# Taking one modulation row off TensorE: multiplied on ScalarE, added on GpSimd

## The chip, the cores and the metric

One core of one Trainium2 chip runs the kernel. It has five engines with an instruction queue each: TensorE (PE in the profile, its weight loads PEld), VectorE (DVE), ScalarE (ACT), GpSimd (POOL) and SyncE (SP), which only issues DMAs here. They share an on-chip memory, SBUF, and TensorE sums into another, PSUM. The engines order their work by semaphores alone. The metric is the device time of one execution in microseconds (us).

## The reference

One layer of a diffusion backbone, for 128 context tokens and 256 latent tokens together, width 2048. Cut to what matters here:

```
def modulation(cvec, w_mod, b_mod):
    m = jax.nn.silu(cvec) @ w_mod + b_mod           # w_mod: 2048 x 12288
    return m.reshape(cvec.shape[0], N_MOD, 1, D_MODEL)

def trunk_layer(x, mod, ...):
    hn = rmsnorm(x, g[0]) * (1.0 + mod[:, 1]) + mod[:, 0]
    z = hn @ w_in                                   # then convolutions, RG-LRU scans, gates
    m = jnp.concatenate([lru_out, sc_out], axis=-1) @ w_out
    x = x + mod[:, 2] * m
    hn = rmsnorm(x, g[1]) * (1.0 + mod[:, 4]) + mod[:, 3]
    f = (jax.nn.silu(hn @ w_gate) * (hn @ w_up)) @ w_down
    x = x + mod[:, 5] * f
```

There are two conditioning vectors (context and latent), so the modulation is a product of 2 x 2048 with 2048 x 12288. It is bound by reading 96 MB of weights, not by arithmetic.

## The kernel before

**Tokens and weights.** All 384 tokens are the columns of every large matmul. Each large weight matrix is worked off in blocks of 1024 columns of SBUF. A block is loaded by SP into a `raw` tile, rounded to `w_hi` on ScalarE (`round_blocks`, L633), its remainder `w_lo = raw - w_hi` is formed on VectorE (`subtract_blocks`, L967), and TensorE makes 24 matmuls of it (L1583 to L1585: hi*hi, hi*lo, lo*hi). Four blocks of `w_hi`/`w_lo` exist, so ScalarE may be at most four blocks ahead: it waits for `block_done`, TensorE for `lo_ready`. Eight blocks make a step.

**The stretch of this case.** Steps are counted as in the code: steps 1 to 7 are part of the input product, step 8 (i = 0) to step 11 (i = 3) are the four output steps, the product with `w_out`. After block 3 and after block 7 of an output step a pair of 128-row tiles is finished. VectorE adds it to the residual stream (`residual_pair`, L1377), ScalarE squares it (`square_pair`, L821), and VectorE adds the squares up (`add_pair`, L1386 and L1387). In ScalarE's program a square stands between the rounding of blocks: r0 r1, square, r2 r3 r4 r5, square, r6 r7. So the rounding of block 6 waits behind a square, and that behind the residual of the pair that TensorE finished last.

**The modulation beside it.** The 12288 columns of `w_mod` are 24 rows of 512 (`m`). Rows 8 to 23 are summed while the large products run, in three ways:

- On TensorE: `mod_units`. One unit is a load of 1 MB (issued by GpSimd, L570) and four matmuls of 512 columns that lie beside each other in the array (`mod_matmuls`, L1613). Row 8 to 11 are 16 such units, rows 14, 16 and 18 (`PE_ROWS`) four units each; one unit stands behind block 3 and one behind block 7 of a step. Row 18 stands in steps 9 and 10. Rows 20 to 22 (`late_mods`) come after it.
- On VectorE: `SIDE_ROWS`, six rows, each as four units of eight instructions (`side_half`, L988: `sums = rows * cond + sums`, 128x512), put between the subtractions of `w_lo` by `SIDE_AT` (`subtract_beside`). Steps 9 and 10 hold three units each, step 11 one. Their loads are also issued by GpSimd (L585). A finished row of partial sums is added up over the partitions by TensorE (`sum_side`, L1664, four matmuls of 256 columns).
- Every row is then copied (`copy_row`), turned (`turn_row`: four matmuls, L1692, or two, L1684, for a side row) and gets its bias (`add_bias`), in the order of `EVENTS`.

GpSimd's program is one queue of DMA issues; each first waits until its buffer is free. VectorE's, ScalarE's and TensorE's programs are equally strict in order.

Of the kernel before, what the change touches and what calls it, by code (L numbers as in the profile page):

```python
# [63 lines left out]
def build(nc, x_prompt, x_sample, state_rglru, c, c_ctx, w_mod, b_mod, norm_g, w_in, lru_conv_w, lru_conv_b,  # L64
# [57 lines left out]
    PE_ROWS = [MOD_FIRST + 4 + r for r in (2, 4, 6)]  # L122
# [6 lines left out]
    SIDE_OPS = 8  # L129
    N_X3 = KT  # L130
# [15 lines left out]
    with ExitStack() as ctx:  # L146
# [110 lines left out]
        side_summed = sem("side_summed")  # L257
        zeroed = sem("zeroed")
# [135 lines left out]
        def side_sums(part):  # L394

            at = 8 * T if part == 5 else 2 * BANK * (part - 3)
            home = token_rows[:] if part < 3 else scratch[:, at:at + 2 * BANK]
            return home.rearrange("p (a n) -> p a n", a=2)

# [140 lines left out]
        def _(pool):  # L540
# [45 lines left out]

            load_gates(0)
# [6 lines left out]
            for step in range(1, HEADS + OUT_STEPS - 1):  # L594
# [3 lines left out]
                if len(units) == 3:  # L598
                    load_side(units[1])
# [6 lines left out]
                load_mod(7 + 2 * step)  # L606
            load_side(SIDE_UNITS - 1)
            for unit in range(LATE_UNITS):
# [3 lines left out]
                elif LATE_SLOTS[unit] == 0:  # L612
                    pool.wait_ge(mod_used, LATE_USED)
                elif LATE_SLOTS[unit] < 3:
                    pool.wait_ge(side_step, SIDE_OPS * (SIDE_UNITS - 2 + LATE_SLOTS[unit]))
                else:
                    pool.wait_ge(act_ready, 2 * (KT // 2))
# [8 lines left out]
        def _(act):  # L626
# [195 lines left out]

            def out_step(n, i, first):
# [27 lines left out]
            with act.Fori(1, OUT_STEPS) as i:  # L851
# [103 lines left out]
        def _(dve):  # L955
# [45 lines left out]
            def copy_row(event):  # L1001

                m = EVENTS[event]
                if m in SIDE_ROWS:
                    dve.wait_ge(side_summed, SIDE_ROWS.index(m) + 1)
# [10 lines left out]
            def add_bias(event):  # L1016
# [9 lines left out]
                elif m in SIDE_ROWS:  # L1026
# [553 lines left out]
        def _(pe):  # L1580
# [77 lines left out]
            def sum_side(part):  # L1658

                sums = side_sums(part)  # L1660
                pe.wait_ge(side_step, 4 * SIDE_OPS * (part + 1))
                pe.wait_ge(mod_ready, LEAD_COUNT + EVENTS.index(SIDE_ROWS[part]))
# [15 lines left out]
            def turn_row(event):  # L1678
# [3 lines left out]
                if EVENTS[event] in SIDE_ROWS:  # L1682
# [13 lines left out]
            def usual(step):  # L1696

                def after(b):
# [7 lines left out]
                    if b % 4 == 3 and step:  # L1706
# [316 lines left out]
```

## Time and profile before

| what | value |
|---|---|
| time, median of 3 runs | 1750.77 us (1750.06 to 1751.92) |
| the profiled execution: its own time | 1751.09 us |
| the profiled execution: its span | 1749.3 us |
| TensorE busy | 1710.8 us of the span |
| VectorE, ScalarE, GpSimd busy | 945.4, 609.8, 63.3 us |
| output steps, as TensorE runs them | about 465 to 613 us of the span |

The span is the time from the first to the last instruction of the profiled execution; its own time is 1.8 us more. The start of a row is what places matmuls: their ends are modelled, and they overlap, so the distance of two starts is what an instruction costs TensorE. A percentage or a busy time of a whole run says little about one stage, so what follows looks at the stretch from 485 to 613 us.

### The profile page before, as it was taken

The numbers are of one execution on the slowest core, as the hardware profiler recorded it, in microseconds if no ns is written. First come the engines' busy times: TensorE is split into PE (matmuls) and PEld (weight loads), VectorE is DVE, ScalarE is ACT, GpSimd is POOL, SyncE is SP. The second block draws the span as 40 slices with busy tenths as digits, with TensorE's granted clock in tenths as the row PEclk, the third lists the DMA queues.
The fourth block names the chain that finished last, engine by engine and source line by source line (L and its number), as shares of the span: only waits on it lengthen the run. The fifth ranks groups of instructions, "written<-read, shape, count | busy, mean of one in ns | idle before, by whom it ended". The sixth has DMA issues, their size and how long they took to land.

```text
span 1749.3 us, 24522 instructions
## 1 busy us (share of the span) xinstructions
PE 1710.8 (98%) x10063; PEld 1632.9 (93%) x10063; DVE 945.4 (54%) x1405; ACT 609.8 (35%) x701; POOL 63.3 (4%) x99
## 2 busy tenths in 40 slices
PE   5999999999999999999999999999999999999997
PEld 3678999999899979999999999999999999999997
DVE  4446678777778578343534434353534435353445
ACT  3333455456523253222222222323232222223235
POOL 2000100110010110000000000000000000000000
PEclk8999999999999999999999999999999999999999
DMA  9996655576677876343334333433333334333421
GB/s 362 379 358 223 239 207 199 201 239 206 212 241 268 289 254 228 121 134 132 120 120 135 129 120 121 136 127 120 121 136 127 120 123 137 124 120 122 141 74 73
DMA packets 206268, 307.56 MB, mean 176 GB/s; under 512 B 5500, under 2 KB 151216, under 8 KB 203776
## 3 DMA queue, kind: packets, MB, share of 16 engines
q1 hardware_dynamic: 189472, 237.07, 40.2%
q0 software_dynamic: 16528, 69.63, 11.1%
q8 instruction: 43, 0.70, 0.2%
q14 instruction: 17, 0.14, 0.0%
q10 hardware_dynamic: 208, 0.02, 0.0%
HBM read 303.55 MB, written 3.15 MB: 175 GB/s over the span
## 4 chain that ended last, share of the span: by engine, by line
PE 94%; DMA 2%; DVE 2%; ACT 1%; issue 0%; SPq 0%; ACTq 0%; DVEq 0%
PE psum L1583 30%; PE psum L1585 29%; PE psum L1584 29%; PE psum L1613 1%; DMA raw<-in_w_mod 1%; DMA scratch<-in_w_in 1%; PE psum L1627 1%; PE psum L1605 1%; PE psum L1638 0%; DVE scratch L1182 0%; PE psum L1920 0%; PE psum L1692 0%; DVE stage L1123 0%; DVE act_lo L1399 0%; ACT scratch L668 0%
## 5 line engine op out<-in xcount | busy, mean ns | idle before, releaser
L967 DVE TENSOR_TENSOR w_lo<-raw,w_hi 128x1024 fp32r<-128x1024 f32 x364 | 444.2, 1224 | 643.3 <-ACT w_hi L633 642.8
L1583 PE MATMUL psum<-act_hi,w_hi 128*128 128x384 f32 x2304 | 775.0, 336 | 5.6 <-DVE act_lo L1139 3.3
L1585 PE MATMUL psum<-act_hi,w_lo 128*128 128x384 f32 x2304 | 770.6, 334 | 0.0
L1584 PE MATMUL psum<-act_lo,w_hi 128*128 128x384 f32 x2304 | 770.4, 334 | 0.0
L633 ACT ACTIVATE w_hi<-raw 128x1024 fp32r<-128x1024 f32 x364 | 381.6, 1058 | 790.8 <-PE psum L1585 718.6
L1583 PEld LDWEIGHTS psum<-act_hi,w_hi 128*128 128x128 f32 x2304 | 432.8, 188 | 35.0 <-issue 25.8
L1584 PEld LDWEIGHTS psum<-act_lo,w_hi 128*128 128x128 f32 x2304 | 433.0, 188 | 0.0
L1585 PEld LDWEIGHTS psum<-act_hi,w_lo 128*128 128x128 f32 x2304 | 432.9, 188 | 0.0
L1583 PE MATMUL psum<-h_hi,w_hi 128*128 128x384 f32 x704 | 235.8, 335 | 0.9 <-DVE h_lo L1443 0.9
L1585 PE MATMUL psum<-h_hi,w_lo 128*128 128x384 f32 x704 | 235.2, 334 | 0.0
L1584 PE MATMUL psum<-h_lo,w_hi 128*128 128x384 f32 x704 | 235.2, 334 | 0.0
L1583 PEld LDWEIGHTS psum<-h_hi,w_hi 128*128 128x128 f32 x704 | 132.1, 188 | 1.2 <-DVE h_lo L1443 1.2
L1584 PEld LDWEIGHTS psum<-h_lo,w_hi 128*128 128x128 f32 x704 | 132.2, 188 | 0.0
L1585 PEld LDWEIGHTS psum<-h_hi,w_lo 128*128 128x128 f32 x704 | 132.1, 188 | 0.0
L1452 DVE SCALAR_TENSOR_TENSOR xT<-psum,modT,xT 128x128 f32<-128x128 f32 x352 | 122.1, 410 | 6.8 <-PE psum L1585 6.7
L988 DVE SCALAR_TENSOR_TENSOR token_rows<-raw,cond,token_rows 128x512 f32<-128x512 f32 x90 | 61.6, 745 | 0.0
L988 DVE SCALAR_TENSOR_TENSOR scratch<-stage,cond,scratch 128x512 f32<-128x512 f32 x62 | 42.4, 746 | 0.0
L1627 PE MATMUL psum<-raw,cond_w 128*32 128x512 f32 (+1 forms) x288 | 36.3, 593 | 4.7 <-DMA raw<-in_w_mod 4.7
L866 ACT ACTIVATE h_hi<-stage 128x768 fp32r<-128x768 f32 x22 | 18.6, 847 | 51.6 <-DVE stage L1438 51.6
L821 ACT ACTIVATE scratch<-xT 128x768 f32 (+1 forms) x8 | 6.8, 847 | 79.9 <-DVE xT L1377 79.9
L1117 DVE TENSOR_TENSOR w_lo<-scratch,w_hi 128x768 fp32r<-128x768 f32 x16 | 15.1, 955 | 26.8 <-ACT w_hi L654 26.8
L654 ACT ACTIVATE w_hi<-scratch 128x768 fp32r<-128x768 f32 x16 | 13.2, 836 | 39.9 <-DMA scratch<-in_w_in 36.8
(189 smaller groups left out, 758.4 us busy)
## 6 DMA issues: line engine op xcount, KB each, us to landing
raw<-in_w_mod POOLq DMA_DIRECT2D x50, 1024.0 KB, 6.1
raw<-in_w_gate SPq DMA_DIRECT2D x44, 1024.0 KB, 5.0
raw<-in_w_up SPq DMA_DIRECT2D x44, 1024.0 KB, 5.0
raw<-in_w_down SPq DMA_DIRECT2D x44, 1024.0 KB, 5.0
raw<-in_w_in SPq DMA_DIRECT2D x34, 1024.0 KB, 5.2
raw<-in_w_mod SPq DMA_DIRECT2D x32, 1024.0 KB, 9.4
raw<-in_w_out SPq DMA_DIRECT2D x16, 1024.0 KB, 5.5
stage<-in_w_mod POOLq DMA_DIRECT2D x14, 1024.0 KB, 6.5
```

The costliest lines, as they stand in the source:

```text
L633: act.activation(split_view(w_hi, b), source, ACT.Copy).then_inc(hi_ready, 1)
L866: act.activation(h_hi[:, 2 * pair:2 * pair + 2, :], silu_g[:, 2 * pair:2 * pair + 2, :], ACT.Copy)\
L967: dve.tensor_tensor(split_view(w_lo, b), source, split_view(w_hi, b).bitcast(F32), ALU.subtract).then_inc(lo_ready, 1)
L988: dve.scalar_tensor_tensor(sums[:, a, :], rows[:, j, :], cond[:, a, k:k + 1], sums[:, a, :], ALU.mult, ALU.add).then_inc(side_step, 1)
L1117: dve.tensor_tensor(w_lo[k % SLOTS][:, 0:X_WIDE], x_raw[k % 2], w_hi[k % SLOTS][:, 0:X_WIDE].bitcast(F32), ALU.subtract).then_inc(lo_ready, 1)
L1452: last = dve.scalar_tensor_tensor(xT[:, k, start:end], psum[:, down_banks[j] + a, start:end], modT[:, 5 * KT + k, seg:seg + 1], xT[:, k, s ...
L1583: pe.matmul(psum[:, bank, 0:T], hi, x_hi, start=first, stop=False)
L1584: pe.matmul(psum[:, bank, 0:T], hi, x_lo, start=False, stop=False)
L1585: return pe.matmul(psum[:, bank, 0:T], lo, x_hi, start=False, stop=last)
L1605: out = pe.matmul(psum[32 * j:32 * j + 32, MOD_BANK, :], cond_w[:, k, :], rows[:, 512 * j:512 * j + 512], start=k == 0, stop=k == KT - 1, ...
L1613: out = pe.matmul(psum[32 * j:32 * j + 32, MOD_BANK, :], cond_w[:, 4 * q + j, :], rows[:, j, :], start=q == 0, stop=q == 3, tile_position= ...
L1627: out = pe.matmul(psum[32 * j:32 * j + 32, MOD_BANK, 0:tiles * P], cond_w[:, depth * unit + i, :], rows[:, i, :], start=unit == 0 and i < ...
```

## The change

Row 18 leaves `PE_ROWS` and becomes `SHARED_ROW`. Its eight loads of 512 KB (two of 16 k each) are issued by ScalarE. ScalarE multiplies each piece by the conditioning values (`scale_shared`: four activations of 128x512 with a per-partition scale for each of eight groups, 32 in all), GpSimd adds the products into `shared_sums` (`add_shared`: four additions of 128x512 a group, two for the first, 30 in all), and TensorE adds up over the partitions as for a side row. Group g + 2 is loaded when group g has been multiplied; group g + 1 is multiplied when group g has been added. In steps 9 and 10 the four `mod_units` fall away. GpSimd's additions stand in its queue between the loads of the side rows. Row 18 is turned in the short form. ScalarE's loop over the output steps is written out.

```
-    PE_ROWS = [MOD_FIRST + 4 + r for r in (2, 4, 6)]
+    PE_ROWS = [MOD_FIRST + 4 + r for r in (2, 4)]
+    SHARED_ROW = MOD_FIRST + 4 + 6
+    SUM_ORDER = SIDE_ROWS[:4] + [SHARED_ROW] + SIDE_ROWS[4:]
...
+        shared_raw = [stage[:, (4 + b) * BLOCK:(5 + b) * BLOCK].rearrange("p (k n) -> p k n", n=512) for b in (0, 1)]
+        shared_scaled_rows = stage[:, 0:2 * BLOCK].rearrange("p (k a n) -> p k a n", k=2, a=2)
+        shared_sums = scratch[:, 4 * BANK:6 * BANK].rearrange("p (a n) -> p a n", a=2)
...
+            def add_shared(group):
+                for k in range(2):
+                    if group == 0 and k == 0:
+                        continue
+                    for a in range(2):
+                        pool.wait_ge(shared_scaled, scaled_until(group) + 2 * k + a + 1)
+                        done = added_until(group) + (2 * k if group else 0) + a
+                        if done >= 2:
+                            pool.wait_ge(shared_added, done - 1)
+                        pool.tensor_tensor(shared_sums[:, a, :], shared_sums[:, a, :], shared_scaled_rows[:, k, a, :],
+                                           ALU.add).then_inc(shared_added, 1)
...
-            for step in range(1, HEADS + OUT_STEPS - 1):
+            for step in range(1, HEADS + 1):
...
+            load_side(13)
+            load_side(14)
+            add_shared(0)
+            add_shared(1)
+            add_shared(2)
+            load_side(15)
+            add_shared(3)
+            load_side(16)
+            add_shared(4)
+            load_side(17)
+            add_shared(5)
+            add_shared(6)
+            load_side(18)
+            add_shared(7)
             load_side(SIDE_UNITS - 1)
...
+            def load_shared(group):
+                if group < 2:
+                    act.wait_ge(act_ready, KT // 2 + 4)
+                else:
+                    act.wait_ge(shared_scaled, scaled_until(group - 1))
+                act.dma_start(shared_raw[group % 2],
+                              w_mod_v[:, 2 * group:2 * group + 2, SHARED_ROW * 512:SHARED_ROW * 512 + 512])\
+                    .then_inc(shared_landed[group % 2], 16)
+
+            def scale_shared(group):
+                if group == 0:
+                    act.wait_ge(act_ready, 2 * (KT // 2))
+                    act.wait_ge(head_done, HEADS)
+                else:
+                    act.wait_ge(shared_added, added_until(group))
+                act.wait_ge(shared_landed[group % 2], 16 * (group // 2 + 1))
+                for k in range(2):
+                    for a in range(2):
+                        to = shared_sums[:, a, :] if group == 0 and k == 0 else shared_scaled_rows[:, k, a, :]
+                        at = 2 * group + k
+                        act.activation(to, shared_raw[group % 2][:, k, :], ACT.Copy, scale=cond[:, a, at:at + 1])\
+                            .then_inc(shared_scaled, 1)
+                if group + 2 < SHARED_GROUPS:
+                    load_shared(group + 2)
...
                 else:
                     round_blocks("GM", n, range(0, 2))
+                    if i < 3:
+                        scale_shared(4 * i - 3)
                     square_pair(i * 2 - 1)
                     round_blocks("GM", n, range(2, 4))
+                    if i < 3:
+                        scale_shared(4 * i - 2)
+                if first:
+                    load_shared(0)
+                    load_shared(1)
                 round_blocks("GM", n, range(4, 6))
+                if 0 < i < 3:
+                    scale_shared(4 * i - 1)
                 square_pair(i * 2)
                 round_blocks("GM", n, range(6, 8))
+                if i < 2:
+                    scale_shared(4 * i)
...
+                if part == len(SIDE_ROWS):
+                    pe.wait_ge(shared_added, added_until(SHARED_GROUPS))
+                    pe.wait_ge(mod_ready, LEAD_COUNT + EVENTS.index(SHARED_ROW))
...
-                    if b % 4 == 3 and step:
+                    if b % 4 == 3 and step > HEADS:
+                        pass
+                    elif b % 4 == 3 and step:
                         mod_units(6 + 2 * step + b // 4, 7 + 2 * step + b // 4)
...
+                    elif b == 7 and step >= 3 and EVENTS[step - 3] == SHARED_ROW:
+                        sum_side(len(SIDE_ROWS))
```

GpSimd's queue from the loads of step 8 to the last side row. L570 are loads of units for TensorE (`mod_units`), L585 loads of side units, L620 loads of the late rows. Before:

```order
66 L570 DMA raw<-in_w_mod 128x4x512 x2
67 L585 DMA stage<-in_w_mod 128x4x512
68 L585 DMA raw<-in_w_mod 128x4x512
69 L570 DMA raw<-in_w_mod 128x4x512
70 L585 DMA stage<-in_w_mod 128x4x512
71 L570 DMA raw<-in_w_mod 128x4x512
72 L585 DMA raw<-in_w_mod 128x4x512
73 L585 DMA stage<-in_w_mod 128x4x512
74 L570 DMA raw<-in_w_mod 128x4x512
75 L585 DMA raw<-in_w_mod 128x4x512
76 L570 DMA raw<-in_w_mod 128x4x512
77 L585 DMA stage<-in_w_mod 128x4x512
```

The same place of the changed kernel, where L588, L603 and L665 are the three kinds of load and L615 the additions:

```order
66 L588 DMA raw<-in_w_mod 128x4x512 x2
67 L603 DMA stage<-in_w_mod 128x4x512
68 L603 DMA raw<-in_w_mod 128x4x512
70 L615 TENSOR_TENSOR scratch<-scratch,stage 128x512 x10
71 L603 DMA stage<-in_w_mod 128x4x512
72 L615 TENSOR_TENSOR scratch<-scratch,stage 128x512 x4
73 L603 DMA raw<-in_w_mod 128x4x512
74 L615 TENSOR_TENSOR scratch<-scratch,stage 128x512 x4
75 L603 DMA stage<-in_w_mod 128x4x512
76 L615 TENSOR_TENSOR scratch<-scratch,stage 128x512 x8
77 L603 DMA raw<-in_w_mod 128x4x512
78 L615 TENSOR_TENSOR scratch<-scratch,stage 128x512 x4
```

Four loads of 1 MB are gone, and the side loads stand behind additions instead of behind those loads.

ScalarE in the changed kernel, from the last roundings of step 8 through step 9. L678 rounds a block, L866 squares a pair, L890 multiplies for the shared row, L874 issues its loads:

```order
207 L866 ACTIVATE scratch<-xT 128x768
208 L678 ACTIVATE w_hi<-raw 128x1024 x2
209 L890 ACTIVATE scratch<-stage,cond 128x512 x2
210 L890 ACTIVATE stage<-stage,cond 128x512 x2
211 L874 DMA stage<-in_w_mod 128x2x512
212 L678 ACTIVATE w_hi<-raw 128x1024 x2
213 L890 ACTIVATE stage<-stage,cond 128x512 x4
214 L874 DMA stage<-in_w_mod 128x2x512
215 L866 ACTIVATE scratch<-xT 128x768
216 L678 ACTIVATE w_hi<-raw 128x1024 x2
217 L890 ACTIVATE stage<-stage,cond 128x512 x4
218 L874 DMA stage<-in_w_mod 128x2x512
```

Before, only the rows of L678 and L866 stand there, in the same order. VectorE's program differs by one copy, of 256 columns instead of 512.

## Rows read from the trace of the kernel before

**Rows 1.** The page: busy time by engine, and the chain that ended last
```profile
PE 1710.8 (98%) x10063; PEld 1632.9 (93%) x10063; DVE 945.4 (54%) x1405; ACT 609.8 (35%) x701; POOL 63.3 (4%) x99
PE 94%; DMA 2%; DVE 2%; ACT 1%; issue 0%; SPq 0%; ACTq 0%; DVEq 0%
```

**Rows 2.** Busy time of each engine in the half steps of steps 9 and 10
```profile
core 0: us, PE busy (x) PEld busy (x) DVE busy (x) ACT busy (x) POOL busy (x), PEclk, DMA share, GB/s
502.50:521.30 18.80, 18.80 (x118) 17.84 (x114) 16.53 (x25) 4.76 (x5) 1.50 (x2) 1.00 0.50 168
521.30:539.60 18.30, 18.30 (x117) 17.04 (x113) 14.42 (x23) 4.75 (x5) 2.32 (x4) 1.00 0.86 291
539.60:557.70 18.10, 18.10 (x112) 17.28 (x108) 15.89 (x25) 4.76 (x5) 1.42 (x2) 1.00 0.67 229
```

**Rows 3.** TensorE in order of time: start, length, instruction; around its modulation matmuls
```profile
521.28 0.44 PE L1583 MATMUL psum<-act_hi,w_hi 128*128 128x384 f32 x1
...
537.86 0.34 PE L1585 MATMUL psum<-act_hi,w_lo 128*128 128x384 f32 x1
538.13 1.07 PE L1613 MATMUL psum<-raw,cond_w 128*32 128x512 f32 x8
539.01 0.61 PE L1664 MATMUL psum<-scratch,ones 128*32 128x256 f32 x8
539.56 0.44 PE L1583 MATMUL psum<-act_hi,w_hi 128*128 128x384 f32 x1
...
556.31 0.50 PE L1684 MATMUL psum<-select,mod_row 128*128 128x4 f32 x4
556.75 1.07 PE L1613 MATMUL psum<-raw,cond_w 128*32 128x512 f32 x8
557.74 0.44 PE L1583 MATMUL psum<-act_hi,w_hi 128*128 128x384 f32 x1
...
588.20 0.95 PE L1692 MATMUL psum<-select,mod_row 128*128 128x2 f32 x8
589.01 0.42 PE L1583 MATMUL psum<-act_hi,w_hi 128*128 128x384 f32 x1
```

**Rows 4.** ScalarE in order of time, step 9; in brackets its idle time before
```profile
505.61 2.95 ACT L633 ACTIVATE w_hi<-raw 128x1024 fp32r<-128x1024 f32 x3
511.18 1.06 ACT L633 ACTIVATE w_hi<-raw 128x1024 fp32r<-128x1024 f32 x1 [2.62 <-PE psum L1585]
524.80 0.85 ACT L821 ACTIVATE scratch<-xT 128x768 f32 x1 [12.57 <-DVE xT L1377]
525.56 2.94 ACT L633 ACTIVATE w_hi<-raw 128x1024 fp32r<-128x1024 f32 x3
```

**Rows 5.** VectorE in order of time, step 9
```profile
520.38 2.73 DVE L988 SCALAR_TENSOR_TENSOR scratch<-raw,cond,scratch 128x512 f32<-128x512 f32 x4
...
523.30 1.37 DVE L1377 SCALAR_TENSOR_TENSOR xT<-psum,modT,xT 128x128 f32<-128x128 f32 x4
526.63 1.23 DVE L967 TENSOR_TENSOR w_lo<-raw,w_hi 128x1024 fp32r<-128x1024 f32 x1 [1.96 <-ACT w_hi L633]
...
539.70 0.42 DVE L1006 COPY mod_row<-psum 128x256 f32<-128x256 f32 x1 [1.95 <-PE psum L1664]
```

**Rows 6.** Groups of instructions by line, on GpSimd, ScalarE and VectorE, each shape apart
```profile
L553 POOL MEMSET scratch<- 128x780 f32 x1 | 0.7, 748 | 28.3 <-PE psum L1740 28.3
L541 POOL MEMSET cond_w<- 128x512 f32 x1 | 0.5, 524 | 0.3 <-POOLq L2011 0.3
L642 ACT ACTIVATE h_hi<-gate_w 128x512 fp32r<-128x512 f32 x8 | 5.0, 629 | 0.0
L967 DVE TENSOR_TENSOR w_lo<-raw,w_hi 128x1024 fp32r<-128x1024 f32 x29 | 35.0, 1222 | 15.1 <-ACT w_hi L633 14.9
L988 DVE SCALAR_TENSOR_TENSOR scratch<-stage,cond,scratch 128x512 f32<-128x512 f32 x32 | 21.9, 747 | 0.0
```

**Rows 7.** GpSimd in order of time, and its modulation loads on the page
```profile
514.64 0.75 POOL L585 DMA_DIRECT2D stage<-in_w_mod  x1 [10.98 <-DVE scratch L988]
550.88 0.75 POOL L585 DMA_DIRECT2D raw<-in_w_mod  x1 [10.61 <-DVE scratch L988]
raw<-in_w_mod POOLq DMA_DIRECT2D x50, 1024.0 KB, 6.1
```

More of the change, by code:

```diff
@@ L129, in build @@
     SIDE_OPS = 8
+    SHARED_GROUPS = KT // 2
     N_X3 = KT
@@ L257, in build @@
         side_summed = sem("side_summed")
+        shared_landed = [sem(f"shared_landed{b}") for b in range(2)]
+        shared_scaled = sem("shared_scaled")
+        shared_added = sem("shared_added")
         zeroed = sem("zeroed")
@@ L398, in side_sums, with scaled_until, added_until @@
             return home.rearrange("p (a n) -> p a n", a=2)
+        shared_raw = [stage[:, (4 + b) * BLOCK:(5 + b) * BLOCK].rearrange("p (k n) -> p k n", n=512) for b in (0, 1)]
+        shared_scaled_rows = stage[:, 0:2 * BLOCK].rearrange("p (k a n) -> p k a n", k=2, a=2)
+        shared_sums = scratch[:, 4 * BANK:6 * BANK].rearrange("p (a n) -> p a n", a=2)
+        def scaled_until(group):
+            return 4 * group
+        def added_until(group):
+            return 4 * group - 2 if group else 0
         def late_unit(unit):
@@ L597, in _ @@
                     load_side(units[0])
-                if len(units) == 3:
-                    load_side(units[1])
                 load_mod(6 + 2 * step)
@@ L615, in _ @@
                     pool.wait_ge(side_step, SIDE_OPS * (SIDE_UNITS - 2 + LATE_SLOTS[unit]))
+                elif LATE_SLOTS[unit] == 3:
+                    pool.wait_ge(shared_scaled, scaled_until(SHARED_GROUPS))
                 else:
-                    pool.wait_ge(act_ready, 2 * (KT // 2))
+                    pool.wait_ge(shared_added, added_until(SHARED_GROUPS))
                 landed_sem, _, to = late_unit(unit)
@@ L843, in out_step @@
                     round_blocks("GM", n, range(0, 2))
+                    if i < 3:
+                        scale_shared(4 * i - 3)
                     square_pair(i * 2 - 1)
                     round_blocks("GM", n, range(2, 4))
+                    if i < 3:
[3 more added lines that the diff above has]
+                    load_shared(1)
                 round_blocks("GM", n, range(4, 6))
+                if 0 < i < 3:
+                    scale_shared(4 * i - 1)
                 square_pair(i * 2)
                 round_blocks("GM", n, range(6, 8))
+                if i < 2:
+                    scale_shared(4 * i)
             out_step(N_OUT, 0, True)
-            with act.Fori(1, OUT_STEPS) as i:
+            for i in range(1, OUT_STEPS):
                 out_step(i * 8 + N_OUT, i, False)
@@ L1003, in copy_row @@
                 m = EVENTS[event]
-                if m in SIDE_ROWS:
-                    dve.wait_ge(side_summed, SIDE_ROWS.index(m) + 1)
+                if m in SUM_ORDER:
+                    dve.wait_ge(side_summed, SUM_ORDER.index(m) + 1)
                     dve.tensor_copy(mod_row[:, 0:256], psum[:, SMALL_BANK, 256:512]).then_inc(row_ready, 1)
@@ L1660, in sum_side @@
                 sums = side_sums(part)
-                pe.wait_ge(side_step, 4 * SIDE_OPS * (part + 1))
-                pe.wait_ge(mod_ready, LEAD_COUNT + EVENTS.index(SIDE_ROWS[part]))
+                if part == len(SIDE_ROWS):
+                    pe.wait_ge(shared_added, added_until(SHARED_GROUPS))
+                    pe.wait_ge(mod_ready, LEAD_COUNT + EVENTS.index(SHARED_ROW))
+                else:
+                    pe.wait_ge(side_step, 4 * SIDE_OPS * (part + 1))
+                    pe.wait_ge(mod_ready, LEAD_COUNT + EVENTS.index(SIDE_ROWS[part]))
                 for g in range(4):
```

5 lines of the change are left out of this document (3 added, 2 removed).

## The prediction

> **What bounds the kernel now.** I read the page's busy times and chain first, then the half steps of the output product, then TensorE, ScalarE and VectorE in order of time around one residual. On the page TensorE is busy for 1710.8 of 1749.3 us and makes 94% of the chain that ended last [rows 1]. So a matmul taken out of TensorE's queue shortens the run, as long as nothing else becomes late. The half steps show who is next: where row 18 is summed, TensorE is busy all the time at its full granted clock (1.00), and VectorE is busy 16.53 of 18.80 us, 14.42 of 18.30 and 15.89 of 18.10 us, while ScalarE needs under 5 us of each [rows 2]. ScalarE has room, VectorE next to none.
>
> Averages don't say when VectorE must be ready, so I follow one residual of step 9. VectorE ends its last multiply-add of the side rows at 520.38 + 2.73 = 523.1 us, after TensorE has finished the pair (block 4 starts at 521.28) [rows 3, 5]. The residual starts at 523.30, ScalarE squares at 524.80 and rounds block 6 from 525.56, and VectorE's `w_lo` of it is ready at 526.63 + 1.23 = 527.86 [rows 4, 5]. TensorE runs blocks 4 to 7 from 521.28 to the matmul at 537.86, 96 matmuls with 95 distances in 16.58 us, so a block is 4.2 us, and it takes block 6 at 521.28 + 8.4 = 529.7 [rows 3]. VectorE's whole lead at this point is 1.8 us. It is given back once a step: VectorE sits idle for 1.95 us up to 539.70, until TensorE has summed a side row [rows 5].
>
> **What TensorE saves.** Four units go. A unit holds TensorE from its start to the next one's: 538.13 to 539.01 is 0.88 us with a sum behind it, 556.75 to 557.74 is 0.99 us with a block behind it [rows 3]. That is 3 x 0.99 + 0.88 = 3.85 us. Added is one more sum over partitions, 539.01 to 539.56, 0.55 us [rows 3]. The turn of row 18 takes the short form, 556.31 to 556.75 (0.44 us) instead of 588.20 to 589.01 (0.81 us): 0.37 us less [rows 3]. Sum: 3.85 - 0.55 + 0.37 = 3.7 us. The changes between kinds of matmul cost some tenths too, so I allow 3.3 to 4.4.
>
> **What ScalarE gets.** 32 activations of 128x512. The nearest row of that size takes 629 ns [rows 6], so 20 us over two and a half steps, 5 us a half step. It has the room where it matters: in step 9 the four for group 3 fall behind block 5, at 512.2 us, where ScalarE then waits for 12.57 us for VectorE's residual [rows 4]. Those between blocks 3 and 4 push back block 4 by 2.5 us, but block 5, which waits for TensorE until 511.18, hardly moves [rows 4]. The square and block 6, on which the lead of 1.8 us rests, stand ahead of the next group. Cost: nothing. If the cover were gone, 2.5 us a group.
>
> **What the loads get.** Four loads of 1 MB by GpSimd become eight of 0.5 MB by ScalarE, the same bytes. One is issued two groups, about 18 us, before its use; 1 MB takes 6.1 us to land [rows 7]. Hidden. GpSimd's side loads now stand behind additions. The one at 514.64 us waits for VectorE anyway (10.98 us), the one at 550.88 too (10.61 us) [rows 7]; by ScalarE's times the additions ahead of them end within a microsecond of that, and the blocks that use them come 10 us later. The late rows' first load moves ahead, since its unit of TensorE is gone. The final sum needs the additions by 574 us; they are due at about 556. All at nothing.
>
> **What GpSimd gets, and VectorE with it.** 30 additions of two SBUF operands, 128x512. No row shows GpSimd reading SBUF; what it has is MEMSETs: 524 ns for 512 columns, 748 ns for 780 [rows 6]. The slope is 224 / 268 = 0.84 ns a column, with 0.1 us fixed. Two reads a column at that pace give 0.96 us, two reads and a write 1.38 us. I take 1.15. GpSimd alone has time for them: 8 in a half step are 9.2 of 18.3 us.
>
> The open price is what such an addition does to VectorE. Its instructions here, the subtraction (1222 ns) and the side rows' multiply-add (747 ns), each read two SBUF operands [rows 6]; GpSimd's read two as well. From 506.7 to 523 us VectorE runs such instructions without a gap, so if anything on the way to SBUF is shared, the addition costs VectorE its share in full. Below, an addition costs VectorE nothing; above, its whole 1.38 us. A gain for VectorE is excluded, since it sheds only half a copy. By ScalarE's times groups 0 and 1 are added between 490 and 500 us, where VectorE is mostly idle. Groups 2 to 7, 24 additions, fall beside VectorE's dense stretches. Of those I count five as free (they meet one of the gaps, such as the 1.96 us before 526.63, or a residual, which reads PSUM) [rows 5]. Also free are the lead, 1.8 us, and the wait of 1.95 us. With a hold of h per addition the kernel gets longer by 19 h - 3.75 - 0.4 us, where the 0.4 is the short turn, the one saving that comes after the stretch; the units' saving is lost while TensorE waits for VectorE. It breaks even at h = 0.22 us and costs 0.2% at h = 0.40. I take h = 1.0, between the two reads alone (2 x 512 x 0.84 ns = 0.86 us) and the whole addition (1.15): 19 - 4.15 = 14.9 us.
>
> The Trainium skill, page "SBUF — State Buffer", section "Who interferes with whom", says that a VectorE instruction with two SBUF inputs contends with a GpSimd instruction that reads SBUF, and that the one that starts second is blocked until the first is through. No trace here can agree or disagree yet; by that rule h would be the whole addition. The page "GPSIMD Engine Reference", section "Performance versus the Vector engine", gives 4497 ns for an addition of 2048 fp32 columns; a quarter of it, 1.12 us, is an estimate from that page, and with it the sum would be 17 us.
>
> **The sum.** Against the profiled execution's own 1751.1 us: 1751.1 + 14.9 = 1766.0. The median of the runs is 0.3 us lower, so **1765.7 us**, 0.85% slower.
>
> **Rivals.**
>
> *Nothing is shared* (chance 0.30). VectorE runs at its old durations beside the additions, and the 3.7 us of TensorE come through: 1750.8 - 3.7 = 1747.1 us. For it: VectorE's program is unchanged, and each other price above is covered. Against it: it needs h below 0.1 us, on an engine whose lead is 1.8 us.
>
> *GpSimd is slow by itself* (0.05). ScalarE multiplies a group only when the last is added. If an addition takes over 18.3 / 8 = 2.3 us, the four of a group don't fit between two groups, ScalarE stands in front of a rounding, and TensorE waits for `w_hi`. At 3 us an addition, three half steps lose 8 x 0.7 = 5.6 us each, less a cover of some 5 us: about 1762 us. Against it: the MEMSETs' pace.
>
> *A hold, but a small one* (0.03), 0.1 to 0.4 us an addition: 1748 to 1754 us.
>
> *The row's last sum comes late*, so that the change doesn't do what it says: additions that end after 574 us hold up TensorE itself, 1 us for 1 us. It would take 18 us of delay that TensorE does not share, so I give it no chance of its own and count it with the slow GpSimd.
>
> **How the numbers follow.** VectorE held by more than 0.4 us an addition: 0.62. Its own range goes from h = 0.6 (7 us) to h = 1.38 (22 us): 1758 to 1773. The two ends, nothing and the full length, are not told apart by any row; taken as evenly spread between 0 and 1.38 us, the part above 0.40 is 0.7, and I set some of it aside for engines that share nothing at all. A measurement of this kernel tells about 0.2%, 3.5 us, from no change. Sharing nothing gives 3.7 us, just past that, so its 0.30 splits into 0.20 faster and 0.10 the same; the small hold adds 0.02 to the same and 0.01 to slower. Slower: 0.62 + 0.05 + 0.01 = 0.68, same 0.12, faster 0.20. The cases have both signs, so the range must hold both: from 1746.2 (a saving of 4.4 us) to 1775, which leaves out a hold longer than the addition itself, about 1 in 10.
>
> **What the profile of the changed kernel will show.** If the hold is right: additions on GpSimd beside VectorE's subtractions, one or both longer than alone; the multiply-add's mean over 747 ns or gaps before it; TensorE waiting in steps 9 and 10 for `w_lo` or a residual, which it doesn't do now; step 11 as before. The additions of group 1, beside an idle VectorE, give their length alone (0.96 to 1.38 us). If nothing is shared: VectorE's means at 747 and 1222 ns, the half steps at 17.2 to 17.8 us without a wait. ScalarE's activations should be near 0.63 us, and its idle time before the squares shrink from 12.6 to about 10 us. Wrong would be made by additions under 0.4 us of hold, or by VectorE always going first, with GpSimd taking only its gaps.

## The result, and the profile after

The changed kernel takes **1773.78 us** (median of 4 runs, 1773.45 to 1774.19) against 1750.41 us for the kernel before (4 runs, 1749.65 to 1751.92): ratio 1.0131, interval 1.0119 to 1.0143, so 23.4 us more. Slower was forecast, and the time lies within the range, 8 us above the value predicted.

The page of the changed kernel, to be read against [rows 1]: busy time by engine, the chain that ended last, and three groups of instructions (busy us, mean ns of one, idle time before).

```profile
PE 1715.3 (97%) x10035; PEld 1639.7 (93%) x10035; DVE 975.2 (55%) x1405; ACT 629.8 (36%) x733; POOL 104.3 (6%) x125
...
PE 90%; DVE 6%; DMA 2%; ACT 1%; issue 1%; SPq 0%; ACTq 0%; DVEq 0%
...
L1666 PE MATMUL psum<-act_hi,w_hi 128*128 128x384 f32 x2304 | 779.6, 338 | 24.4 <-DVE w_lo L1050 18.7
...
L1071 DVE SCALAR_TENSOR_TENSOR scratch<-stage,cond,scratch 128x512 f32<-128x512 f32 x62 | 48.6, 845 | 0.0
L615 POOL TENSOR_TENSOR scratch<-scratch,stage 128x512 f32<-128x512 f32 x30 | 44.0, 1498 | 23.8 <-ACT stage L890 23.7
```

VectorE has the same 1405 instructions as before and is busy 29.8 us longer. Its share of the chain went from 2% to 6%, and TensorE now waits 18.7 us for `w_lo`, where it did not wait before. The half steps show where, against [rows 2] (the stretches are no longer exactly half steps, since all of it is later):

```profile
502.50:521.30 18.80, 17.30 (x102) 16.81 (x100) 16.90 (x16) 9.77 (x13) 10.00 (x8) 1.00 0.44 138
521.30:539.60 18.30, 13.79 (x67) 13.50 (x68) 16.40 (x21) 5.84 (x8) 5.90 (x5) 0.81 0.49 168
539.60:557.70 18.10, 11.78 (x56) 10.76 (x56) 17.74 (x16) 4.18 (x7) 9.31 (x8) 0.81 0.54 178
557.70:575.60 17.90, 14.31 (x85) 14.22 (x83) 16.30 (x12) 9.41 (x13) 11.87 (x9) 0.96 0.51 170
575.60:597.00 21.40, 18.58 (x92) 18.61 (x93) 19.44 (x29) 4.71 (x5) 3.24 (x4) 0.80 0.55 185
```

From 539.6 to 557.7 us VectorE is busy for 17.74 of 18.10 us and TensorE for 11.78, with 56 matmuls where the kernel before ran 112. Two pieces of step 9 show how the time is lost. VectorE in order of time, against [rows 5]:

```profile
506.80 5.86 DVE L1071 SCALAR_TENSOR_TENSOR scratch<-stage,cond,scratch 128x512 f32<-128x512 f32 x4
512.58 2.31 DVE L1050 TENSOR_TENSOR w_lo<-raw,w_hi 128x1024 fp32r<-128x1024 f32 x1
514.81 2.73 DVE L1071 SCALAR_TENSOR_TENSOR scratch<-stage,cond,scratch 128x512 f32<-128x512 f32 x4
517.46 0.55 DVE L1469 TENSOR_TENSOR token_rows<-token_rows,scratch 128x384 f32<-128x384 f32 x1
518.04 5.92 DVE L1470 TENSOR_TENSOR token_rows<-token_rows,scratch 128x384 f32<-128x384 f32 x1
```

GpSimd over the same time, and its group 1, which stands beside a VectorE that has little to do:

```profile
494.56 6.12 POOL L615 TENSOR_TENSOR scratch<-scratch,stage 128x512 f32<-128x512 f32 x4 [0.99 <-ACT stage L890]
...
507.26 6.55 POOL L615 TENSOR_TENSOR scratch<-scratch,stage 128x512 f32<-128x512 f32 x4 [6.58 <-ACT stage L890]
517.84 0.76 POOL L603 DMA_DIRECT2D stage<-in_w_mod  x1 [4.03 <-DVE scratch L1071]
518.61 4.93 POOL L615 TENSOR_TENSOR scratch<-scratch,stage 128x512 f32<-128x512 f32 x4
```

Beside group 2, four multiply-adds take 5.86 us instead of 2.73 and the subtraction behind them 2.31 instead of 1.22; in between, where no addition runs, four take 2.73 again. Beside group 3 a single addition of squares (L1470), 0.56 us long otherwise, takes 5.92 us: it spans all four additions, which run back to back in 4.93 us. Both pictures cost VectorE the same: 3.13 + 1.09 + 5.36 = 9.58 us for eight additions. Worked out the same way groups 4 and 5 cost 9.57 us, and 6 and 7 9.54 us: 28.7 us for 24 additions, **1.20 us each**, with none free. (Beside groups 0 and 1 two instructions of VectorE are 1.6 us longer in sum, where it has time for it; with these the 29.8 us of the page are accounted for to half a microsecond.)

TensorE meets it in the middle of the step, and for the last and longest time in the middle of step 10:

```profile
519.35 0.95 PE L1779 MATMUL psum<-select,mod_row 128*128 128x2 f32 x8
525.37 0.66 PE L1666 MATMUL psum<-act_hi,w_hi 128*128 128x384 f32 x1 [5.06 <-DVE w_lo L1050]
525.82 0.52 PE L1667 MATMUL psum<-act_lo,w_hi 128*128 128x384 f32 x1
526.14 0.52 PE L1668 MATMUL psum<-act_hi,w_lo 128*128 128x384 f32 x1
...
578.42 0.66 PE L1666 MATMUL psum<-act_hi,w_hi 128*128 128x384 f32 x1 [6.41 <-DVE w_lo L1050]
...
598.50 0.45 PE L1666 MATMUL psum<-act_hi,w_hi 128*128 128x384 f32 x1
```

After the wait of 5.06 us two starts are 0.32 us apart instead of 0.174: the granted clock is at the lower level (0.50 from 522.9 to 529.6 us, that is 1.2 GHz). It is so for 12, 16 and 17 matmuls behind three such waits, and the mean of the half steps falls to 0.80 and 0.81.

The matmul at 578.42 us is the one that started at 557.74 us before [rows 3], so TensorE is 20.7 us late there. The one at 598.50 us started at 575.58 us before: 22.9 us. Between the two TensorE waits for no `w_lo`; the 2.2 us come from the matmuls at the lower clock. The subtraction that the first of them waits for, before and after:

```profile
551.68 1.23 DVE L967 TENSOR_TENSOR w_lo<-raw,w_hi 128x1024 fp32r<-128x1024 f32 x1
```

```profile
577.04 1.23 DVE L1050 TENSOR_TENSOR w_lo<-raw,w_hi 128x1024 fp32r<-128x1024 f32 x1
```

### The profile page after: what moved, and what is told of

Its sections match the earlier page's. It is cut to its first block, busy times and chain, and to the rows that moved or that the text cites. A ratio compares the mean times of both kernels' runs of the same rounds, so it can differ in the third digit from the quotient of the medians.

```text
span 1771.7 us, 24545 instructions
## 1 busy us (share of the span) xinstructions
PE 1715.3 (97%) x10035; PEld 1639.7 (93%) x10035; DVE 975.2 (55%) x1405; ACT 629.8 (36%) x733; POOL 104.3 (6%) x125
## 3 DMA queue, kind: packets, MB, share of 16 engines
q0 software_dynamic: 15440, 65.44, 10.4%
## 4 chain that ended last, share of the span: by engine, by line
PE 90%; DVE 6%; DMA 2%; ACT 1%; issue 1%; SPq 0%; ACTq 0%; DVEq 0%
PE psum L1666 29%; PE psum L1668 28%; PE psum L1667 28%; DVE scratch L1071 2%; PE psum L1696 1%; DMA scratch<-in_w_in 1%; DVE token_rows L1470 1%; PE psum L1710 1%; PE psum L1688 1%; DVE w_lo L1050 1%; DMA raw<-in_w_mod 1%; PE psum L1721 0%; DVE scratch L1265 0%; PE psum L2011 0%; DVE xT L1460 0%
## 5 line engine op out<-in xcount | busy, mean ns | idle before, releaser
L1666 PE MATMUL psum<-act_hi,w_hi 128*128 128x384 f32 x2304 | 779.6, 338 | 24.4 <-DVE w_lo L1050 18.7
L678 ACT ACTIVATE w_hi<-raw 128x1024 fp32r<-128x1024 f32 x364 | 381.6, 1058 | 785.7 <-PE psum L1668 705.5
L1071 DVE SCALAR_TENSOR_TENSOR scratch<-stage,cond,scratch 128x512 f32<-128x512 f32 x62 | 48.6, 845 | 0.0
L615 POOL TENSOR_TENSOR scratch<-scratch,stage 128x512 f32<-128x512 f32 x30 | 44.0, 1498 | 23.8 <-ACT stage L890 23.7
L866 ACT ACTIVATE scratch<-xT 128x768 f32<-128x768 f32 x8 | 6.8, 846 | 82.7 <-DVE xT L1460 82.7
```

The costliest lines, as they stand in the source:

```text
L615: pool.tensor_tensor(shared_sums[:, a, :], shared_sums[:, a, :], shared_scaled_rows[:, k, a, :], ALU.add).then_inc(shared_added, 1)
L678: act.activation(split_view(w_hi, b), source, ACT.Copy).then_inc(hi_ready, 1)
L1071: dve.scalar_tensor_tensor(sums[:, a, :], rows[:, j, :], cond[:, a, k:k + 1], sums[:, a, :], ALU.mult, ALU.add).then_inc(side_step, 1)
L1666: pe.matmul(psum[:, bank, 0:T], hi, x_hi, start=first, stop=False)
```

## The experiments

Times and ratios are against runs of the kernel before on the same chip. All but those of 5 start from the changed kernel.

**1. GpSimd writes and reads nothing.**

```
-  pool.tensor_tensor(shared_sums[:, a, :], shared_sums[:, a, :], shared_scaled_rows[:, k, a, :], ALU.add)
+  pool.memset(shared_sums[:, a, :], 0.0)
```

> The changed kernel with each of GpSimd's 30 additions replaced by a MEMSET of 128x512, which writes SBUF and reads nothing (row 18 of the modulation is left out of the result by it). Theory (GpSimd's reads hold VectorE): no VectorE instruction is lengthened, TensorE never waits in steps 9 and 10, and only its saving is left: 1750.4 - 3.7 = 1746.7 us, within 1 us. Rival 1 (any use of SBUF by GpSimd holds VectorE): 24 MEMSETs of 0.52 us cost 12.5 us, less 3.75 of cover and 0.4 saved: about 1758.8 us. Rival 2 (ScalarE's 32 multiplications, its loads or GpSimd's changed queue make the time): 1773 us as before.

Measured: 1746.89 us against 1750.43, ratio 0.9977 (0.9967 to 0.9987). GpSimd and VectorE by group:

```profile
L615 POOL MEMSET scratch<- 128x512 f32 x30 | 15.4, 540 | 28.2 <-ACT stage L889 27.1
...
L1070 DVE SCALAR_TENSOR_TENSOR scratch<-stage,cond,scratch 128x512 f32<-128x512 f32 x62 | 42.4, 747 | 0.0
```

VectorE is back at 747 ns beside 30 writes of GpSimd, and TensorE never waits for `w_lo`. All else of the change is in this kernel: the loads, ScalarE's 32 activations, the semaphores, the sum. So these cost nothing that shows, TensorE's saving comes to 3.5 us, and the additions cost 26.9 us.

**2. One read in place of two, and half the width.** A copy of the scaled row; in another run additions of 256 columns (the other half isn't added).

```
+  pool.tensor_copy(shared_sums[:, a, :], shared_scaled_rows[:, k, a, :])                        # run 2a
+  pool.tensor_tensor(shared_sums[:, a, 0:256], shared_sums[:, a, 0:256], ...[:, k, a, 0:256])   # run 2b
```

> The changed kernel with each addition replaced by a copy of 128x512 by GpSimd: one read and one write instead of two reads and one write (row 18 is wrong in the result). Theory (a read by GpSimd holds VectorE for the length of GpSimd's instruction): a copy takes 0.5 to 0.8 us, 24 of them 12 to 19 us, less 4.2: 1758 to 1765 us, and VectorE's two-operand instructions are lengthened by one copy each. Rival (only the second read collides, or only one read stream is shared): 1747 us.

> The changed kernel with additions of 256 columns instead of 512, as many of them (half of row 18's columns are left out). Theory (VectorE loses the whole length of each addition): an addition takes about 0.65 us, VectorE loses 24 x 0.65 = 15.6 us, less 4.2: 1761.8 us, within 2 us. Rival (the cost is per instruction, or from something else in the change): 1770 us or more.

Measured: 1754.94 us, ratio 1.0026 (1.0016 to 1.0035) for the copy; 1758.94 us, ratio 1.0043 (1.0027 to 1.0060) for half the width. The copies:

```profile
L615 POOL COPY scratch<-stage 128x512 f32<-128x512 f32 x30 | 29.8, 1029 | 24.4 <-ACT stage L889 24.4
...
L1070 DVE SCALAR_TENSOR_TENSOR scratch<-stage,cond,scratch 128x512 f32<-128x512 f32 x62 | 45.6, 797 | 0.0
```

Less reading on GpSimd, less delay, and with only writes (1) none, so it is its reads. Half the width came out 0.9 us under its expected range. For the copy the expectation missed by 3 us: beside group 2 four multiply-adds take 3.79 us, a quarter of a microsecond more each, so a copy holds VectorE for less than its own 0.6 to 1.6 us.

**3. VectorE's side.** Two of its side rows are summed in two free PSUM banks, so that these multiply-adds have one SBUF operand; the last one writes SBUF.

```
+                acc = psum[:, 4:6, :] if part in (3, 4) else sums
...
+  dve.scalar_tensor_tensor((sums if k == KT - 1 else acc)[:, a, :], rows[:, j, :], cond[...], acc[:, a, :], ...)
```

> The changed kernel, whole, but VectorE's side rows 17 and 19 are summed in two idle PSUM banks and go to SBUF with the last multiply-add only, so that 60 of each row's multiply-adds read one SBUF operand instead of two. Theory (GpSimd's addition holds only VectorE instructions with two SBUF operands): multiply-adds of the rows in PSUM keep 0.75 us beside an addition, subtractions and the adding of squares are still held; about 10 us of the 28.7 us that VectorE lost are left, less 4.2 of cover: 1754 to 1764 us. Rival (GpSimd's addition holds whatever VectorE does): 1773 us.

Measured: 1760.87 us, ratio 1.0059 (1.0043 to 1.0076). By group, and VectorE in order of time in step 9:

```profile
L1072 DVE SCALAR_TENSOR_TENSOR psum<-stage,cond,psum 128x512 f32<-128x512 f32 x28 | 19.1, 748 | 0.0
...
507.18 2.73 DVE L1072 SCALAR_TENSOR_TENSOR psum<-stage,cond,psum 128x512 f32<-128x512 f32 x4
509.81 1.46 DVE L1050 TENSOR_TENSOR w_lo<-raw,w_hi 128x1024 fp32r<-128x1024 f32 x1
...
515.00 6.07 DVE L1050 TENSOR_TENSOR w_lo<-raw,w_hi 128x1024 fp32r<-128x1024 f32 x1
```

GpSimd's instructions are the same, and multiply-adds with a PSUM operand keep their 748 ns beside them. So do those that read their sum from PSUM and write it to SBUF: two such, from 537.37 us on, take 0.73 us each beside an addition that starts at 537.26 us. It is VectorE's second read of SBUF that matters here, not its write. What is held are the subtractions, with two SBUF operands; three of them wait for a whole group of four additions (6.07, 6.00 and 6.10 us).

**4. ScalarE's work taken away** (activations of one column).

```
-  act.activation(to, shared_raw[group % 2][:, k, :], ACT.Copy, scale=...)
+  act.activation(to[:, 0:1], shared_raw[group % 2][:, k, 0:1], ACT.Copy, scale=...)
```

> The changed kernel with every activation of the moved row cut from 512 columns to 1 (the row is then not scaled; the loads, the semaphores and GpSimd's 30 additions are as they were). Theory (the extra time comes from GpSimd's reads of SBUF beside VectorE alone): 1772 to 1775 us, the changed kernel's 1773.8. Rival (ScalarE's 20 us of activations delay its roundings or squares, and so VectorE and TensorE): the time falls by several us, towards 1765.

Measured: 1773.85 us, ratio 1.0127 (1.0110 to 1.0144). The activations fell from 0.71 to 0.28 us and the time did not move. ScalarE has no part in it.

This run shows one more thing, since its additions begin a little earlier. The first two multiplications of a side row (L1067) read one SBUF operand and write SBUF; in the changed kernel they run just ahead of group 6, here beside it. The changed kernel, then this run:

```profile
560.41 0.87 DVE L1067 TENSOR_SCALAR scratch<-raw,cond 128x512 f32<-128x512 f32 x2
```

```profile
560.48 3.04 DVE L1067 TENSOR_SCALAR scratch<-raw,cond 128x512 f32<-128x512 f32 x2
```

They are held too, 1.61 and 1.51 us each instead of 0.48. So one SBUF operand alone does not make an instruction safe.

**5. The same additions elsewhere, in the kernel before.** Thirty additions that belong to nothing, in the MLP steps, in one row or 8.3 us apart (the second form waits at each `e`, the first only at `e == 0`).

```
+            for e in range(30):
+                pool.wait_ge(lo_ready, N_LOOP + 8 + 2 * e)
+                if e >= 2:
+                    pool.wait_ge(extra_added, e - 1)
+                pool.tensor_tensor(scratch[:, at:at + 512], scratch[:, at:at + 512], cond_w[...], ALU.add)
```

> The kernel before with 30 additions of 128x512 on GpSimd that belong to nothing, issued back to back in the MLP steps, where VectorE runs a subtraction of 1.23 us in every 4.16 us and is 43% busy. Theory (one VectorE instruction with two SBUF operands is passed over by a whole row of additions that follow each other without a gap): a row of 30 x 1.23 = 37 us holds VectorE, TensorE has about three rounded blocks (12 us) ahead of it and waits about 25 us, so 1770 to 1778 us. Rival (the two engines alternate, one for one): each addition delays VectorE by 1.2 us at most, 9 subtractions in the stretch lose 11 us of 26 us of idle time, and the time stays at 1750.4.

> The same 30 additions on the kernel before, but each waits for a later w_lo subtraction of the MLP steps (every second one), so that they stand 8.3 us apart. Theory (an addition costs nothing where VectorE has idle time for it, 1.2 us against 2.93 us free per block): 1750.4 us, ratio 1.000. Rival (each addition costs its 1.2 us wherever it stands): 30 x 1.2 = 36 us more, 1786 us.

Measured: in a row 1750.77 us, ratio 0.9998 (0.9988 to 1.0008); apart 1751.24 us, ratio 1.0001 (0.9991 to 1.0010). My theory for the row fell. GpSimd and VectorE in that run:

```profile
751.24 1.29 POOL L630 TENSOR_TENSOR scratch<-scratch,cond_w 128x512 f32<-128x512 f32 x1 [69.32 <-DVE w_lo L977]
752.50 1.27 POOL L630 TENSOR_TENSOR scratch<-scratch,cond_w 128x512 f32<-128x512 f32 x1
753.74 1.28 POOL L630 TENSOR_TENSOR scratch<-scratch,cond_w 128x512 f32<-128x512 f32 x1
754.99 2.27 POOL L630 TENSOR_TENSOR scratch<-scratch,cond_w 128x512 f32<-128x512 f32 x1
...
754.09 2.02 DVE L977 TENSOR_TENSOR w_lo<-raw,w_hi 128x1024 fp32r<-128x1024 f32 x1 [1.63 <-ACT w_hi L642]
```

The subtraction that comes at 754.09 us waits for the third addition to end (755.02) and runs till 756.11; the fourth addition is held meanwhile. The engines take turns. In this stretch VectorE has room, 19.1 idle us of 40 in the kernel before (745 to 785 us; it is busy for 52%, not the 43% of the expectation), and each of 30 additions is free. Nor is it the moment of the start that makes a long wait: at 783 us a subtraction starts 0.02 us behind an addition (though not the first of its row), just as the three of (3) do, and waits for that one only:

```profile
783.19 1.29 POOL L630 TENSOR_TENSOR scratch<-scratch,cond_w 128x512 f32<-128x512 f32 x1
783.21 2.36 DVE L977 TENSOR_TENSOR w_lo<-raw,w_hi 128x1024 fp32r<-128x1024 f32 x1 [2.38 <-ACT w_hi L642]
```

**6. What makes one instruction wait for four.** Either a short gap between additions (each waits for the one just before it), or the three loads that stood right ahead of groups 3, 5 and 7 put behind them.

```
-                        if done >= 2:
-                            pool.wait_ge(shared_added, done - 1)
+                        if done:
+                            pool.wait_ge(shared_added, done)      # the gap
...
+            pool.wait_ge(side_step, SIDE_OPS * (side_before(15)[0] + 1))
             add_shared(3)
+            load_side(15)                                         # the order; the same for 17, 18
```

> The changed kernel, with each addition waiting for the end of the addition just before it and not of the one before that, which puts a short gap between two additions of a row. Theory A (a waiting VectorE instruction slips in at any gap): the subtraction and the sum of squares that were held 5.9 us over four additions are held about 1.3 us, the work behind them then meets the other additions one for one, the sum of the holds stays near 24 x 1.2 us, and the time stays within 1770 to 1774 us. Theory B (the gap lets VectorE run beside what was lost): 1765 to 1769 us. Rival (no difference in the rows): 5.9 us stays, 1773.8 us.

> The changed kernel with the three loads of VectorE's rows that GpSimd issues just ahead of groups 3, 5 and 7 issued behind these groups; the additions wait for the same count as the load did, so they start at the same place of the program. The rows so far show one VectorE instruction held over four additions only where a load was issued right ahead of them (six places in two kernels), and one for one elsewhere (30 additions in a row with no load ahead held no subtraction for more than one). Theory (the load ahead is what makes the difference): the sums of squares that took 5.9 us take 1.8 us or less in all three places, and VectorE and GpSimd alternate; the sum of holds stays, so 1770 to 1774 us. Rival (the place in VectorE's order makes it): 5.9 us stays.

Measured: with the gap 1771.26 us, ratio 1.0119 (1.0102 to 1.0136); with the order 1768.18 us, ratio 1.0104 (1.0089 to 1.0119). The addition of squares of step 9 and the subtraction behind it, with the gap and then with the order:

```profile
518.62 2.28 DVE L1470 TENSOR_TENSOR token_rows<-token_rows,scratch 128x384 f32<-128x384 f32 x1
520.93 2.17 DVE L1050 TENSOR_TENSOR w_lo<-raw,w_hi 128x1024 fp32r<-128x1024 f32 x1
```

```profile
518.48 1.53 DVE L1473 TENSOR_TENSOR token_rows<-token_rows,scratch 128x384 f32<-128x384 f32 x1
520.05 2.17 DVE L1053 TENSOR_TENSOR w_lo<-raw,w_hi 128x1024 fp32r<-128x1024 f32 x1
```

Either one ends the long wait, in all three places. But gapless and behind a load is not enough. The half-width run of (2) has both, in the same place, and there the addition of squares is held for one addition only:

```profile
517.17 0.76 POOL L603 DMA_DIRECT2D stage<-in_w_mod  x1 [4.04 <-DVE scratch L1071]
517.38 1.04 DVE L1470 TENSOR_TENSOR token_rows<-token_rows,scratch 128x384 f32<-128x384 f32 x1
```

So the nine long waits on record (three each in the changed kernel, in (3) and in (4)) all stand at a gapless group of four additions of 512 columns with a load right ahead of it. A gap, the load moved away, or 256 columns end them. Why is not shown. Nor does the load by itself hold VectorE: in step 11 of the changed kernel an addition of squares beside a load takes its 0.56 us (596.12 us). The run with the order changed also moved the additions' start against VectorE (0.42 us before the addition of squares instead of 0.57 us behind it), so that the load alone made the difference there is not fully shown.

Breaking the row gives back 3 and 6 of the 23 us, since VectorE meets the other three additions one by one: step 9 costs it 8.94 us (gap) and 8.20 us (order) in place of 9.58. The second run came out 2 us under what was expected.

**7. The additions on VectorE itself**, 15 of 128x1024.

```
+  dve.tensor_tensor(shared_sums, shared_sums, shared_scaled_rows[:, k, :, :], ALU.add).then_inc(shared_added, 2)
```

> The changed kernel with the additions made by VectorE itself, 15 of 128x1024 (one of two halves), two of them behind a block's work in each half step; ScalarE still multiplies and loads. A subtraction of 128x1024 costs VectorE 1.22 us, so 15 cost 18.3 us or 4.9 us in a half step with 4.7 us idle, against 1.2 us for each of 24 held, 28.7 us, when GpSimd adds. Theory (a GpSimd addition costs VectorE twice its own way of doing it): VectorE is just full in the half steps, TensorE waits 0 to 6 us, against 3.5 us saved: 1747 to 1754 us. Rival (VectorE's order, with ScalarE chained to it, makes TensorE wait as long as now): 1765 us or more.

Measured: 1764.91 us, ratio 1.0078 (1.0064 to 1.0092). My theory fell; this is the rival's 1765 us. The group, and VectorE around the next residual:

```profile
L1075 DVE TENSOR_TENSOR scratch<-scratch,stage 128x1024 f32<-128x1024 f32 x15 | 18.3, 1222 | 0.9
...
528.00 1.37 DVE L1466 SCALAR_TENSOR_TENSOR xT<-psum,modT,xT 128x128 f32<-128x128 f32 x4
531.23 1.23 DVE L1042 TENSOR_TENSOR w_lo<-raw,w_hi 128x1024 fp32r<-128x1024 f32 x1 [1.85 <-ACT w_hi L670]
```

VectorE does the work in 18.3 us, where GpSimd's doing it costs VectorE 28.7 us. But I had counted all of its idle time, 4.7 us a half step, as room, and it isn't: behind each residual VectorE waits 1.85 us for the square and the rounding that depend on it, wherever the step stands. The prediction's cover gives the right sum here: 18.3 - 3.75 - 0.4 = 14.2 us, measured 13.7.

**8. Both mended.** PSUM sums (3) with the gap (6); and that once more with each addition as two of 256 columns.

```
+                        pool.tensor_tensor(shared_sums[:, a, 0:256], ..., ALU.add).then_inc(shared_half, 1)
+                        pool.wait_ge(shared_half, done + 1)
+                        pool.tensor_tensor(shared_sums[:, a, 256:512], ..., ALU.add).then_inc(shared_added, 1)
```

> The run with side sums in PSUM (two of VectorE's rows of multiply-adds no longer have two SBUF operands, 1760.9 us) together with the gap between additions. The subtractions held over four additions (6.1 to 7.1 us, four places) were what TensorE then waited for (10.9 us in all). Theory (a gap lets a held instruction in after one addition, and what follows it in these steps has a PSUM operand and is not held): each of the four loses at most 1.3 us in place of 4.9, TensorE's waits fall to about 2 us, 1749 to 1754 us. Rival (the held total is shifted to the next two-operand instructions as in the run with gaps alone, which gained only 2.5 us): 1757 to 1760 us.

> The run with two side sums in PSUM and a gap between additions (1752.8 us), with each addition made as two of 256 columns with a gap between these too. There a subtraction held by an addition took 1.6 to 2.4 us in place of 1.2, and TensorE still waited 3.7 us for them (before: 0). Theory (a hold ends with the addition that is running, so half the length makes half the hold): subtractions of 1.5 to 1.9 us, TensorE waits 0 to 2 us, 1749 to 1751.5 us, level with or a little under the kernel before. Rival (twice as many starts hold VectorE as long or longer in sum): subtractions stay at 2.3 us in places and the time at 1752 to 1755 us.

Measured: 1752.77 us, ratio 1.0008 (0.9999 to 1.0018), and 1751.85 us, ratio 1.0004 (0.9995 to 1.0013). TensorE's waits for `w_lo` in the first and the second (us in all, how many, the longest):

```profile
PE psum L1668 <- DVE w_lo L1050: 3.7, 3, 2.2
```

```profile
PE psum L1672 <- DVE w_lo L1054: 3.4, 3, 2.5
```

22 us of the 23.4 come back without a change to what GpSimd computes. Neither version beats the kernel before: what is left of the holds just eats the saving of 3.5 us. (The expectation speaks of four long waits in (3); its trace has three, the 7.1 us being two subtractions together.) Halving the additions made the held subtractions shorter (1.35 to 1.76 us instead of 1.64 to 2.38) but held more of them, 5.3 us in sum instead of 5.8. The waits fell by 0.3 us, to 3.4, where 2 us or less were expected, and the times can't be told apart; the second lies just over its expected 1751.5.

## Why the prediction was right, point by point

- **What bounds it**: right. TensorE had no slack and VectorE a lead of 1.8 us and a wait of 1.95 us a step. As a number the cover of 3.75 us fits all runs to within 2.4 us, also one in which GpSimd adds nothing (7). As a mechanism it is too small, as the point on the cover says.
- **What TensorE saves**: 3.7 us predicted, 3.5 measured (1), within the 3.3 to 4.4.
- **ScalarE and the loads, at nothing**: right in sum (1, 4), though an activation takes 0.71 us and not 0.63. The idle time before a square did not shrink from 12.6 to 10 us but grew to 16.9 in step 9, since the residual it waits for is late. ScalarE also waited three times for GpSimd, 8.1 us in all, but TensorE never waited for `w_hi` in this stretch.
- **GpSimd's addition**: 1.15 us taken, 1.25 to 1.29 us where nothing holds it, inside the bounds of 0.96 and 1.38. Group 1, which I named as the place to read it, shows it with one disturbance: its first addition meets a subtraction (2.37 us), the other three take 1.28 us each.
- **The hold, the term that was mis-sized.** The mechanism was right: (1) shows that it is GpSimd's reads, (3) that it is VectorE's second read of SBUF, with the exception seen in (4). The term was 19 h with h = 1.0, since five of the 24 additions were counted as free. Measured are 24 additions at 1.20 us, 28.7 us: nearly a whole addition each, and none free. The five were meant to meet a gap or a residual of VectorE. By the trace none does: ScalarE's products come behind a rounding, and so GpSimd starts only when VectorE is in its dense stretch again (the gaps end at 505.65, 535.08 and 559.27 us, the next groups start at 507.26, 536.69 and 560.88 us).
- **The sum.** With the measured term it is 28.7 - 3.75 - 0.4 = 24.5 us; measured 23.4. The same holds for the other runs, with what the additions of groups 2 to 7 cost VectorE, worked out from each trace (in (7), where it makes the additions itself, all 15):

| run | what VectorE loses, us | less 4.15 | measured |
|---|---|---|---|
| copies (2) | 8.8 | 4.6 | 4.5 |
| half width (2) | 12.0 | 7.9 | 8.5 |
| sums in PSUM (3) | 15.2 | 11.1 | 10.4 |
| gap (6) | 25.7 | 21.6 | 20.2 |
| order (6) | 23.5 | 19.3 | 16.9 |
| on VectorE (7) | 18.3 | 14.2 | 13.7 |
| PSUM and gap (8) | 5.8 | 1.7 | 1.5 |
| the same, halves (8) | 5.3 | 1.1 | 1.0 |

- **The cover.** Part of this agreement is luck. The lead of 1.8 us was read at one residual, but TensorE waits last, and longest, for the subtraction at 577.04 us. Before, it stood at 551.68 us and was ready at 552.91 us, 4.8 us ahead of its use at 557.74 us. VectorE is 25.4 us late at it and TensorE behind it 20.7 us, so 8.0 of the 28.7 us were covered by then, not 3.75. Of the 4.2 us of difference some 2 came back through the clock, which the prediction left out; the other 2 are what the sum has too much (24.5 us against 22.4 between the two profiled spans).
- **The rule of the Trainium skill**, page "SBUF — State Buffer", section "Who interferes with whom", by which the second of two such instructions is blocked until the first is through: the traces agree, with 2.02 us for a subtraction of 1.23 us that came 0.93 us before an addition's end (5). It says nothing of a row that passes a waiting instruction over, which the rows show (5.92 us). The estimate of 1.12 us an addition from the Trainium skill's page "GPSIMD Engine Reference", section "Performance versus the Vector engine", is a little under the 1.25 to 1.29 us of the trace.
- **Rivals.** Nothing shared: refuted as a whole, though its time, 1747.1 us, is what the kernel takes once GpSimd doesn't read (1746.9). GpSimd slow by itself: refuted, 1.29 us against the 2.3 it would need. A small hold is what a copy makes (2). The last sum late: the final addition ends at 576.6 us by then, and TensorE, itself late, did not wait for it.
- **The clock**, not foreseen: the lower level behind three waits makes about 45 matmuls 0.15 us longer, some 7 us. Behind the first two TensorE waits for VectorE again, so those 4 us should be given back in shorter waits; that is argued and was not tried apart. Behind the third it waits no more, and the 17 matmuls' 2.5 us are paid: they are the 2.2 us by which TensorE is later at 598.50 us than at 578.42 us.

## What to carry to other kernels

An engine that moves work off the critical one may still be paid for by a third: before giving GpSimd work on SBUF, look at what VectorE runs beside it, and count each addition as its full length for VectorE if that has two SBUF operands. In these runs the same work cost nothing where VectorE had real slack or read one of its operands from PSUM. And idle time in an average is not room: only the lead over the engine that waits, and the waits that a delay would shorten, are.

## What the runs showed of the hardware that I had not expected

- A VectorE instruction can be passed over by a whole gapless row of GpSimd additions: 5.92 us for one of 0.56 us, nine times in three kernels, each time with a load issued by GpSimd right ahead of a row of 512-column additions. It was held from 518.04 us on, 0.57 us before the first addition starts by the trace. Thirty additions in a row without such a load passed over none (2.36 us at most), and neither did additions of 256 columns behind a load (1.04 us).
- A GpSimd MEMSET holds VectorE not at all (747 ns stay), and a copy for much less than its own length.
- A multiply-add with its sum in PSUM costs VectorE no more (748 ns) than one in SBUF (747 ns).
- A TENSOR_SCALAR with one SBUF operand, written to SBUF, is held by an addition too (1.61 us instead of 0.48, run 4); written to PSUM it took 0.74 us with an addition beside it (run 3).
- The granted clock fell to its lower level during TensorE's waits of 5.06, 3.52 and 6.41 us, and came back 4.3 to 5.9 us after their ends; around one of 2.79 us it stayed at the full level.
